# A two-layer convolutional decoder on eight cores: matmuls of constants in the opening, halved first weight loads, LayerNorm steps spread over two tiles, and a buffer of its own for the last short convolution

## The chip, the cores and the metric

The kernel runs on all 8 NeuronCores of one Trainium2 chip. Each core works on one of eight prompts and on 16 of the 128 sample tokens, with all weights, and the cores exchange nothing. The metric is device time in microseconds of the slowest core. Engines are named as in the profile: PE is TensorE, DVE is VectorE, ACT is ScalarE, POOL is GpSimd, SP is SyncE. POOL and SP also issue the DMA transfers: POOL those with a cast to bf16 (weights) and x tiles 1 to 4, SP and ACT the others.

## The reference

Activations are `D_MODEL = 1024` wide, the prompt has 2048 tokens, the hidden width is `D_FF = 2816`. Two layers, each `x += 0.5*SwiGLU1(RMSNorm(x)); x += Mixer(RMSNorm(x)); x += 0.5*SwiGLU2(RMSNorm(x))`, then a final RMSNorm.

```python
def rms_norm(x, g):
    return x * lax.rsqrt(jnp.mean(x * x, axis=-1, keepdims=True) + RMS_EPS) * g

def swiglu(x, w_gate, w_up, w_down):
    return (jax.nn.silu(x @ w_gate) * (x @ w_up)) @ w_down

def conformer_conv_mixer(x, buf, w_pw1, b_pw1, w_dw, b_dw, ln_g, ln_b, w_pw2, b_pw2):
    a, g = jnp.split(x @ w_pw1 + b_pw1, 2, axis=-1)
    c, new_buf = causal_dwconv(a * jax.nn.sigmoid(g), buf, w_dw)      # width 31
    c = jax.nn.silu(layer_norm(c + b_dw, ln_g, ln_b))
    return c @ w_pw2 + b_pw2, new_buf

def short_gated_conv_mixer(x, buf, w_in, w_conv, w_out):
    b_gate, c_gate, h = jnp.split(x @ w_in, 3, axis=-1)
    c, new_buf = causal_dwconv(c_gate * h, buf, w_conv)               # width 3
    return (b_gate * c) @ w_out, new_buf
```

## The kernel before

The activations X lie in SBUF for the whole run, as 8 chunks of 128 features by 2064 tokens, cut into five tiles of 412 to 416 tokens (`TILES`). Every product is a group of 8 (or 6) bf16 matmuls of 128x128 by 412 columns into one PSUM bank, weights streamed through a ring of six slots (`WRing`) whose loads are issued on POOL in the order of use as slots come free.

The order of every engine's instructions is written out by hand: the Python program emits them in sequence, each engine runs its own in that order, and `P.wait` puts semaphore waits between them.

**RMSNorm.** The class `Norm` makes it: squares on ACT (`sq_chunk`), a running sum of the 8 chunks on POOL, one matmul with `ONES` that sums over the features and spreads the result (`part1b`), `rstd` on ACT (Ln, then Exp), and eight `apply` on DVE, one for each chunk, which PE's products wait for chunk by chunk. `queue_norm` puts a tile's steps in the list `later`, and `pump(n)` takes up to n `apply` from it, after each product.

**The opening** (`start_group`). x tile 0 comes in four pieces on SP, tile 1 and 2 in two pieces each and 3 and 4 in one on POOL. The first load of weights waits for x tile 0's second piece. The sums of squares of tiles 0 to 2 are made on PE, eight matmuls of `ONES` by the squares (`pieces_in`), without POOL. Then products (hj, ti), hidden chunk by token tile: (0,0), (1,0), the norm of tile 1, (0,1), (1,1), (2,0), (3,0), the norm of tile 2, and so on. A product (hj, ti) is 8 matmuls with the gate weights (L584) and 8 with the up weights (L590); its gate is a Silu on ACT and a multiplication on DVE (L601). Six banks rotate, two to a product.

**The first mixer's last stage.** While the depthwise convolution's last chunks are normalised (LayerNorm: `z_mean` and `z_rstd` on DVE, two chunks at a time, then Silu on ACT), the product with `w_pw2` runs: `pw2_item(ti, m)` is 8 matmuls (L939) and an update of X on DVE (L945). During tiles 1 and 2 only four banks rotate, so a product waits for the update four products back. `tail_step(m)` places the rest of the LayerNorm after the products of tile 1, and the next norm's squares and sums are emitted between them.

**The second mixer.** For each chunk c: products with the C and H columns, u = C*h (DVE) into `UR[:, c % 2]`, `conv_stage` (ACT copies u, scaled, into TR, L1154, DVE adds two taps, L1161 and L1169) and, one chunk later, `y_stage` (the product with the B columns, times TR, on DVE, L1186). After the last chunk the output product (`bout_item`, L1236) begins. TR is one buffer, so the copy of chunk 7 waits for `y_stage(6)`.

**The end.** The final norm writes X, and each pair of chunks is stored; in the last tile chunks 6 and 7 go singly.

## Time and profile before

| | |
|---|---|
| median of 3 runs | 2380.83 us (2380.26 to 2380.9) |
| the profiled execution, time / span | 2380.29 us / 2378.5 us (slowest core, core 5) |
| spans of the eight cores | 2372.1 to 2378.5 us |
| granted clock of PE, mean | 0.995 to 0.996 |
| busy: PE / DVE / ACT / POOL | 2336.4 / 937.6 / 576.8 / 442.1 us |

The views are all of core 5. PE's busy time is modelled, so a group of matmuls shows its last one longer than it is; distances between starts are the better measure. The row of a wait gives what released the engine as far as the semaphores show. PEclk is the granted clock, 1.00 being 2.4 GHz and 0.50 1.2 GHz.

### The profile page before, as it was taken

The page shows a single profiled execution, that of the slowest core. Times are in us where ns is not written, and L with a number is a line of the kernel's source. Part 1 is how long each engine was busy: PE and PEld are TensorE (multiplying, and loading weights), DVE is VectorE, ACT ScalarE, POOL GpSimd, SP SyncE. Part 2 cuts the span into 40 slices and gives each one's busy share as a digit, 9 for nine tenths or more (in the row PEclk, how much of TensorE's full clock was granted, in tenths as well). Part 3 has the DMA queues.
Part 4 walks back from the last instruction along what each step waited for, and adds up shares of the span by engine and source line. Part 5 has one row for each costly group of instructions (what it writes and reads, how often), then busy time and mean ns, then how long its engine had stood idle before and what let it go on. Part 6 is the DMA issues. An engine that isn't in the chain of part 4 may idle for free.

```text
span 2378.5 us, 33574 instructions; the slowest of 8 cores (2372.1 to 2378.5 us)
## 1 busy us (share of the span) xinstructions
PE 2336.4 (98%) x14218; PEld 1293.1 (54%) x14218; DVE 937.6 (39%) x1613; ACT 576.8 (24%) x1027; POOL 442.1 (19%) x462
## 2 busy tenths in 40 slices
PE   6999999999999999999999999999999999999997
PEld 2555555555545555555555555555555555555554
DVE  2342232374577242232352423225655634224226
ACT  3401101342475101101341010113322420110123
POOL 1300000340565000000340000004200510000014
PEclk9999999999999999999999999999999999999999
DMA  9243323348402253423333334331434144234325
GB/s 210 31 56 36 45 27 36 36 58 171 81 2 36 27 54 36 44 29 36 37 41 36 40 37 51 36 38 18 56 36 37 20 52 50 33 36 49 35 25 143
DMA packets 187174, 116.44 MB, mean 49 GB/s; under 512 B 8208, under 2 KB 184496, under 8 KB 187024
## 3 DMA queue, kind: packets, MB, share of 16 engines
q0 software_dynamic: 167968, 90.66, 33.2%
q1 hardware_dynamic: 18640, 22.99, 3.6%
q8 instruction: 112, 1.84, 0.3%
q10 hardware_dynamic: 416, 0.64, 0.1%
q14 instruction: 38, 0.31, 0.0%
HBM read 183.29 MB, written 14.88 MB: 83 GB/s over the span
## 4 chain that ended last, share of the span: by engine, by line
PE 93%; DVE 3%; ACT 2%; DMA 1%; POOL 1%; issue 1%; DVEq 0%; SPq 0%; POOLq 0%; ACTq 0%
PE ps L590 26%; PE ps L584 26%; PE ps L629 24%; PE ps L1113 7%; PE ps L1236 2%; PE ps L756 2%; PE ps L750 2%; PE ps L997 2%; PE ps L939 2%; DVE arena L460 1%; DMA arena<-ffn_w_up 0%; PE ps L843 0%; DVE arena L881 0%; DVE arena L632 0%; ACT arena L393 0%
## 5 line engine op out<-in xcount | busy, mean ns | idle before, releaser
L584 PE MATMUL ps<-arena 128*128 128x412 bf16 (+1 forms) x3520 | 693.6, 339 | 8.4 <-DVE arena L460 8.2
L590 PE MATMUL ps<-arena 128*128 128x412 bf16 (+1 forms) x3520 | 688.9, 339 | 1.1 <-DMA arena<-ffn_w_up 1.1
L601 DVE TENSOR_TENSOR arena<-arena,ps 128x412 bf16<-128x412 f32 (+1 forms) x440 | 256.9, 584 | 930.8 <-ACT arena L599 930.7
L629 PE MATMUL ps<-arena 128*128 128x412 bf16 (+1 forms) x3520 | 618.8, 338 | 0.0
L599 ACT ACTIVATE arena<-ps 128x412 f32<-128x412 f32 (+1 forms) x440 | 226.6, 515 | 1352.7 <-PE ps L590 1352.6
L584 PEld LDWEIGHTS ps<-arena 128*128 128x128 bf16 x3520 | 344.9, 98 | 286.7 <-DVE arena L460 15.4
L590 PEld LDWEIGHTS ps<-arena 128*128 128x128 bf16 x3520 | 345.1, 98 | 272.8 <-issue 2.7
L629 PEld LDWEIGHTS ps<-arena 128*128 128x128 bf16 x3520 | 343.7, 98 | 270.5
L632 DVE SCALAR_TENSOR_TENSOR arena<-ps,arena 128x412 f32<-128x412 f32 (+1 forms) x480 | 280.4, 586 | 241.9 <-PE ps L629 241.5
L401 POOL TENSOR_TENSOR arena<-arena 128x412 f32<-128x412 f32 (+3 forms) x222 | 236.2, 1064 | 203.8 <-ACT arena L393 186.6
L460 DVE SCALAR_TENSOR_TENSOR arena<-arena,ps 128x412 bf16<-128x412 f32 (+3 forms) x280 | 170.3, 636 | 92.0 <-ACT ps L453 92.0
L393 ACT ACTIVATE arena<-arena 128x412 f32<-128x412 f32 (+1 forms) x254 | 133.8, 545 | 181.2 <-DVE arena L632 94.4
L1113 PE MATMUL ps<-arena 128*128 128x412 bf16 (+1 forms) x960 | 167.8, 338 | 0.0
L271 POOL DMA_DIRECT2D arena<-ffn_w_gate x44 | 39.0, 887 | 644.0 <-PE ps L590 435.3
L271 POOL DMA_DIRECT2D arena<-ffn_w_down x48 | 41.1, 862 | 588.2 <-PE ps L590 588.2
L1113 PEld LDWEIGHTS ps<-arena 128*128 128x128 bf16 x960 | 93.8, 98 | 73.8
L271 POOL DMA_DIRECT2D arena<-ffn_w_up x44 | 38.9, 885 | 187.1 <-PE ps L629 181.9
L997 PE MATMUL ps<-arena 128*32 128x512 bf16 x1088 | 64.3, 380 | 0.3 <-DVE arena L914 0.3
L939 PE MATMUL ps<-arena 128*128 128x412 bf16 (+1 forms) x320 | 59.9, 344 | 4.7 <-DVE arena L945 4.7
L756 PE MATMUL ps<-arena 128*128 128x412 bf16 (+1 forms) x320 | 62.4, 338 | 0.0
L750 PE MATMUL ps<-arena 128*128 128x412 bf16 (+1 forms) x320 | 62.4, 338 | 0.0
L1236 PE MATMUL ps<-arena 128*128 128x412 bf16 (+1 forms) x320 | 56.7, 338 | 1.8 <-DVE arena L1186 1.8
(79 smaller groups left out, 785.9 us busy)
## 6 DMA issues: line engine op xcount, KB each, us to landing
arena<-ffn_w_gate POOLq DMA_DIRECT2D x44, 512.0 KB, 8.3
arena<-ffn_w_up POOLq DMA_DIRECT2D x44, 512.0 KB, 10.4
arena<-ffn_w_down POOLq DMA_DIRECT2D x32, 512.0 KB, 8.9
yT<-arena SPq DMA_DIRECT2D x16, 412.0 KB, 4.7
arena<-ffn_w_down POOLq DMA_DIRECT2D x16, 384.0 KB, 8.2
arena<-a_w_pw POOLq DMA_DIRECT2D x12, 512.0 KB, 11.5
arena<-b_w_in POOLq DMA_DIRECT2D x12, 512.0 KB, 9.3
vb<-arena SPq DMA_DIRECT2D x8, 512.0 KB, 5.5
```

The source lines that it names most:

```text
L271: tk = P.emit("pool", (lambda e, dst=dst, src=src: e.dma_start(out=dst, in_=src)), waits=[ftk] + gate, sem="w%d" % slot, amount=16)
L393: a = P.emit("act", (lambda e, m=m, t0=t0, w=w, buf=buf: e.activation(out=buf[:, 0:w], in_=X[:, m, t0:t0 + w], func=AF.Square)), waits=[tk ...
L401: self.add_tk[ti, m] = P.emit("pool", (lambda e, w=w, buf=buf, acc=acc, accb=accb, last=last: e.tensor_tensor(out=accb[:, 0:w] if last els ...
L460: d = P.emit("dve", (lambda e, c=c, t0=t0, w=w, dst=dst, gcol=self.gcol, bank=self.rs_bank: e.scalar_tensor_tensor(out=dst[:, c, t0:t0 + w ...
L584: P.emit("pe", (lambda e, k=k, jj=jj, t0=t0, w=w, bg=bg, wgv=wgv: e.matmul(psum[:, bg, 0:w], wgv[:, k, jj * 128:(jj + 1) * 128], XN[:, k, ...
L590: pk = P.emit("pe", (lambda e, k=k, jj=jj, t0=t0, w=w, bu=bu, wuv=wuv: e.matmul(psum[:, bu, 0:w], wuv[:, k, jj * 128:(jj + 1) * 128], XN[: ...
L599: a = P.emit("act", (lambda e, s=s, w=w, bg=bg: e.activation(out=ST[:, s, 0:w], in_=psum[:, bg, 0:w], func=AF.Silu)), waits=[pk, st_free[s]])
L601: dd = P.emit("dve", (lambda e, s=s, w=w, bu=bu, hj=hj, t0=t0: e.tensor_tensor(out=HB[:, hj, t0:t0 + w], in0=ST[:, s, 0:w], in1=psum[:, bu ...
L629: pk = P.emit("pe", (lambda e, jj=jj, mm=mm, t0=t0, w=w, b=b, wdv=wdv, n=n: e.matmul(psum[:, b, 0:w], wdv[:, jj, mm * 128:(mm + 1) * 128], ...
L632: dd = P.emit("dve", (lambda e, m=m, t0=t0, w=w, b=b: e.scalar_tensor_tensor(out=X[:, m, t0:t0 + w], in0=psum[:, b, 0:w], scalar=0.5, in1= ...
L997: pk = P.emit("pe", (lambda e, j=j, g=g, c=c, b=b, sl=sl, n=n: e.matmul(psum[32 * g:32 * g + 32, b, :], DGW[:, sl * 4 + g, j, :], V4[:, c ...
L1113: pk = P.emit("pe", (lambda e, k=k, cc=cc, t0=t0, w=w, bk=bk, wv=wv: e.matmul(psum[:, bk, 0:w], wv[:, k, cc * 128:(cc + 1) * 128], XN[:, k ...
```

## The change

Six edits, taken together.

1. **Opening, weights.** `first_pair` loads the first two weight blocks (g0, u0) by halves of 128 columns, in the order g0, u0, g0, u0, all gated on the first piece of x tile 0 instead of the second. Product (0, ti) waits for the first halves only.
2. **Opening, PE.** `pieces_in` is split: `pieces_sq` (ACT) and `pieces_sum` (PE). After the sums of each piece `warm_up(n)` issues n matmuls of constants (`ONES` by `ONES`) into a bank that nobody reads: 5, 2, 2, 6 after the pieces of tile 0, 0 and 10 for tile 1, none for tile 2. Tile 2's squares are issued two products earlier, all eight `apply` of a tile directly after its `rstd`; the squares of tiles 3 and 4 and the sum of tile 3 one product (or more) earlier.
3. **Squares.** The ring of buffers in `sq_chunk` runs on over the tiles, and chunk 0 takes a ring buffer too, instead of the accumulator. Chunk 0's square no longer waits for the last add of the tile before.
4. **First mixer's last stage.** `tail_step` runs over 16 products (tiles 1 and 2) instead of 8, with at most one call of `ln_dve` each; the norms of tiles 0 and 1 are queued later, and two places without an `apply` stand behind their `rstd`.
5. **Second mixer.** The last short convolution writes into the other half of UR instead of TR (`t_of`).
6. **End.** Chunks 6 and 7 of the last tile are stored as a pair, and ACT issues the pairs (0,1) and (4,5), SP the other two.

```diff
+        def first_pair(self, gate):
+            for half in range(2):
+                for v in range(2):
+                    src, shape, _ = self.units[v]
+                    dst = slot_view(v, shape)
+                    c0 = half * 128
+                    tk = P.emit("pool", (lambda e, dst=dst, src=src, c0=c0: e.dma_start(
+                        out=dst[:, :, c0:c0 + 128], in_=src[:, :, c0:c0 + 128])),
+                        waits=[gate], sem=("w%d" if half else "wh%d") % v, amount=16)
...
-        if ti < 4:
+        if ti == 1:
+            W.first_pair(ld_x[0, 0])
+        elif ti < 4:
...
+        for j in range(n):
+            tk = P.emit("pe", (lambda e, b=b, w=w: e.matmul(
+                psum[:, b, 0:w], ONES, ONES[:, 0:1].broadcast_to([128, w]), start=True, stop=True)),
+                sem="auto" if j == n - 1 else None)
...
-            buf = self.ring[:, 0 if m == 0 else 1 + (m - 1) % nr, :]
+            n = self.nsq
+            self.nsq += 1
+            buf = self.ring[:, 1 + n % nr, :]
...
-            guard = acc_free[0] if m == 0 else (self.add_tk.get((ti, m - nr)) if m > nr else acc_free[0])
+            guard = self.used[n - nr] if n >= nr else acc_free[0]
...
-        norm_in(0)
-        need(0)
+        nrm.pieces_sq(0)
+        norm_in(0, (5, 2, 2, 6))
+        nrm.pieces_sq(1)
         acquire(0)
         waiting = [products(hj, 0) for hj in (0, 1)]
-        norm_in(1)
-        need(1)
+        norm_in(1, (0, 10))
...
-        squares = {7: (3, 0), 9: (3, 4), 10: (4, 0), 12: (4, 4)}
-        sums = {12: 3, 14: 4}
+        squares = {5: (3, 0), 7: (3, 4), 9: (4, 0), 11: (4, 4)}
+        sums = {11: 3, 14: 4}
         for i, (hj, ti) in enumerate(order):
             gate(*products(hj, ti))
+            if i == 1:
+                nrm.pieces_sq(2)
             if i == 3:
-                norm_in(2)
+                norm_in(2, (0, 0))
...
+                if jj == 0:
+                    ltg, ltu = W.half_tk.get(ug, ltg), W.half_tk.get(uu, ltu)
...
-        def tail_step(m):
-            if m == 0:
+        TAIL_LN = {3: 2, 4: 3, 6: 4, 7: 5, 8: 6, 9: 7, 10: 8}
+
+        def tail_step(k):
+            if k == 0:
...
-            elif m == 2:
-                ln_dve(PH - 1, 2)
-            else:
-                for c_ in {3: (3,), 4: (4,), 5: (5, 6), 6: (7, 8)}.get(m, ()):
-                    ln_dve(PH - 1, c_)
-                    ln_act(PH - 1, c_)
+            elif k in TAIL_LN:
+                ln_dve(PH - 1, TAIL_LN[k])
+                if k > 3:
+                    ln_act(PH - 1, TAIL_LN[k])
...
-            sums = {(2, 0): 0, (3, 0): 1, (4, 1): 2, (4, 7): 3}
+            sums = {(2, 3): 0, (3, 2): 1, (4, 1): 2, (4, 7): 3}
...
-                if ti == 1:
-                    tail_step(m)
+                if ti < 3:
+                    tail_step((ti - 1) * KC + m)
                 pump(1)
                 if (ti, m) in sums:
-                    queue_norm(nxt, sums[ti, m])
+                    queue_norm(nxt, sums[ti, m], 2 if ti == 2 else 0)
...
+        def t_of(c):
+            return TR_A if c < KC - 1 else UR[:, c % 2 ^ 1, :]
...
-                out=TR, in_=UR[:, ub, :], func=AF.Copy, scale=WCB[:, c, 2:3])), waits=[du, t_free[0]])
+                out=TR, in_=UR[:, ub, :], func=AF.Copy, scale=WCB[:, c, 2:3])),
+                waits=[du, t_free[0], ubl_tk] if c < KC - 1 else [du, u_free[1 - ub], ubl_tk])
```

The third argument of `queue_norm` (`rest`) adds that many empty entries behind the norm's `rstd`; each uses up one `pump`.

## Rows read from the trace of the kernel before

**Rows 1.** The page's busy times: engine, busy us, share, instructions.

```profile
PE 2336.4 (98%) x14218; PEld 1293.1 (54%) x14218; DVE 937.6 (39%) x1613; ACT 576.8 (24%) x1027; POOL 442.1 (19%) x462
```

**Rows 2.** Waits of PE, whole span: us in total, times, longest.

```profile
PE ps L421 <- ACT arena L416: 11.3, 6, 5.6
PE ps L584 <- DVE arena L460: 8.2, 12, 4.2
PE ps L939 <- DVE arena L945: 4.7, 3, 3.1
```

**Rows 3.** Timeline, first 90 us: start, us, engine, line, operation, [idle before].

```profile
8.60 1.04 POOL L271 DMA_DIRECT2D arena<-ffn_w_gate  x1 [7.91 <-DMA arena<-xT]
...
8.95 0.87 PE L421 MATMUL ps<-arena 128*128 128x412 bf16 x2 [2.49 <-ACT arena L416]
...
16.52 2.90 PE L584 MATMUL ps<-arena 128*128 128x412 bf16 x8 [4.17 <-DVE arena L460]
...
25.57 1.58 ACT L416 ACTIVATE arena<-arena 128x1648 bf16<-128x1648 f32 x1 [1.07 <-DMA arena<-xT]
...
27.18 1.56 PE L421 MATMUL ps<-arena 128*128 128x412 bf16 x8
...
30.02 4.52 DVE L460 SCALAR_TENSOR_TENSOR arena<-arena,ps 128x412 bf16<-128x412 f32 x8 [11.86 <-ACT ps L453]
...
30.72 0.35 PE L584 MATMUL ps<-arena 128*128 128x412 bf16 x1 [1.99 <-DVE arena L460]
...
41.23 1.56 PE L584 MATMUL ps<-arena 128*128 128x412 bf16 x8
...
47.48 3.03 ACT L416 ACTIVATE arena<-arena 128x1648 bf16<-128x1648 f32 x2
...
51.91 2.05 PE L584 MATMUL ps<-arena 128*128 128x412 bf16 x8
...
53.80 1.56 PE L590 MATMUL ps<-arena 128*128 128x412 bf16 x8
...
88.45 0.35 PE L584 MATMUL ps<-arena 128*128 128x412 bf16 x1 [0.21 <-DVE arena L460]
```

**Rows 4.** Windows: PE, PEld, DVE, ACT, POOL busy (x), PEclk, DMA share, GB/s.

```profile
30.70:34.60 3.90, 3.15 (x7) 0.71 (x8) 3.90 (x8) 1.51 (x3) 0.00 (x0) 0.72 1.03 266
...
725.73:729.00 3.27, 3.27 (x11) 1.49 (x12) 3.27 (x7) 1.62 (x3) 2.25 (x3) 0.54 0.00 0
...
733.00:745.50 12.50, 12.50 (x73) 6.99 (x72) 9.71 (x17) 5.95 (x12) 8.01 (x8) 1.00 0.01 2
```

**Rows 5.** DMA queues in 4.6:8, 10.5:16.4, 1676.5:1679 (x, weights, sB): packets, MB, share.

```profile
q1 hardware_dynamic: 463, 0.72, 89.9%
...
q0 software_dynamic: 1513, 0.77, 116.4%
...
q1 hardware_dynamic: 1040, 0.13, 32.5%
```

**Rows 6.** Timeline, the first mixer's last stage.

```profile
706.11 1.21 DVE L871 SCALAR_TENSOR_TENSOR arena<-ps,arena 128x1024 f32<-128x1024 f32 x1
...
718.32 4.35 PE L939 MATMUL ps<-arena 128*128 128x412 bf16 x24 [1.37 <-DVE arena L945]
...
721.99 1.28 ACT L448 ACT_TABLE_LOAD   x1
...
725.04 0.64 DVE L945 SCALAR_TENSOR_TENSOR arena<-ps,arena 128x412 f32<-128x412 f32 x1
...
725.73 7.21 PE L939 MATMUL ps<-arena 128*128 128x412 bf16 x32 [3.06 <-DVE arena L945]
```

**Rows 7.** Timeline, end of the second mixer's convolutions.

```profile
1839.57 2.48 DVE L1161 SCALAR_TENSOR_TENSOR arena<-arena 128x1536 f32<-128x1536 f32 x2 [1.99 <-ACT arena L1154]
...
1845.62 4.69 PE L1236 MATMUL ps<-arena 128*128 128x412 bf16 x26 [1.75 <-DVE arena L1186]
```

**Rows 8.** DMA queue in 2368:2371 (the last outputs).

```profile
q1 hardware_dynamic: 431, 0.66, 109.4%
```

More of the change, by code:

```diff
@@ L379, in __init__ @@
             self.tail_sq = None
+            self.nsq = 0
+            self.used = {}
         def sq_chunk(self, ti, m, tk):
@@ L398, in sq_chunk @@
             acc = self.ring[:, 0, :]
+            a0, in0, n0 = self.sq[ti, m - 1]
+            if m > 1:
+                in0 = acc
             accb = self.accb.get(ti, ACCB)
             bfree = accb_free.get(ti in self.accb) if last else None
-            self.add_tk[ti, m] = P.emit("pool", (lambda e, w=w, buf=buf, acc=acc, accb=accb, last=last: e.tensor_tensor(
-                out=accb[:, 0:w] if last else acc[:, 0:w], in0=acc[:, 0:w], in1=buf[:, 0:w], op=ALU.add)),
-                waits=[self.sq[ti, 0], a, self.add_tk.get((ti, m - 1)), bfree])
+            self.add_tk[ti, m] = self.used[n] = P.emit("pool", (
+                lambda e, w=w, buf=buf, in0=in0, acc=acc, accb=accb, last=last: e.tensor_tensor(
+                    out=accb[:, 0:w] if last else acc[:, 0:w], in0=in0[:, 0:w], in1=buf[:, 0:w], op=ALU.add)),
+                waits=[a0, a, self.add_tk.get((ti, m - 1)), acc_free[0] if m == 1 else None, bfree])
+            if m == 1:
+                self.used[n0] = self.used[n]
             if last:
@@ L406, in sq_chunk, with pieces_sq, pieces_sum @@
                 self.sq[ti] = self.add_tk[ti, m]
-        def pieces_in(self, ti):
+        def pieces_sq(self, ti):
+            t0, w = TILES[ti]
+            n = KC // X_PIECES[ti]
+            self.sq_in = []
+            for j in range(X_PIECES[ti]):
+                c0 = j * n
+                self.sq_in.append(P.emit("act", (lambda e, t0=t0, w=w, c0=c0, n=n: e.activation(
+                    out=SQ[:, c0:c0 + n, 0:w], in_=X[:, c0:c0 + n, t0:t0 + w], func=AF.Square)),
+                    waits=[ld_x[ti, j], sq_free[0]]))
+        def pieces_sum(self, ti, warm):
             t0, w = TILES[ti]
@@ L413, in pieces_in @@
             p1 = None
-            for j in range(X_PIECES[ti]):
-                c0 = j * n
-                a = P.emit("act", (lambda e, t0=t0, w=w, c0=c0, n=n: e.activation(
-                    out=SQ[:, c0:c0 + n, 0:w], in_=X[:, c0:c0 + n, t0:t0 + w], func=AF.Square)),
-                    waits=[ld_x[ti, j], sq_free[0]])
-                P.wait("pe", a)
-                for c in range(c0, c0 + n):
-                    p1 = P.emit("pe", (lambda e, c=c, w=w, bank=bank: e.matmul(
-                        psum[:, bank, 0:w], ONES, SQ[:, c, 0:w], start=(c == 0), stop=(c == KC - 1))),
-                        sem="auto" if c == KC - 1 else None)
+            for c in range(KC):
+                if c % n == 0:
+                    P.wait("pe", self.sq_in[c // n])
+                p1 = P.emit("pe", (lambda e, c=c, w=w, bank=bank: e.matmul(
+                    psum[:, bank, 0:w], ONES, SQ[:, c, 0:w], start=(c == 0), stop=(c == KC - 1))),
+                    sem="auto" if c == KC - 1 else None)
+                if c % n == n - 1:
+                    warm_up(warm[c // n])
             sq_free[0] = p1
@@ L477, in build_program, with queue_norm @@
     later = collections.deque()
-    def queue_norm(nrm, ti):
+    def queue_norm(nrm, ti, rest=0):
         later.append((nrm, ti, -1))
+        for _ in range(rest):
+            later.append((nrm, ti, KC))
         for c in range(KC):
```

49 lines of the change are left out of this document (33 added, 16 removed).

## The prediction, on record before the changed kernel ran

> **What bounds the kernel now.** I read first the busy table of the page: TensorE (PE) is busy for 98% of the span [rows 1], so a change can only win PE's idle time and the time in which PE's clock stands at its lower level. Next the list of waits, which says where PE idles [rows 2]: in the first sums of squares (11.3 us, waiting for ScalarE's squares), before products that wait for VectorE's `apply` (8.2 us), and at three places of the first mixer's last stage (4.7 us); the timeline adds one of 1.75 us before the second mixer's output product [rows 7]. Waits ahead of the first product are mostly the transfers' anyway, so the sum is not to be had whole. I therefore read the timeline at each place [rows 3, 6, 7], and the windows for the clock [rows 4]. A full-rate matmul of 412 columns costs 12.50/73 = 0.17 us, at clock 0.54 it costs 3.27/11 = 0.30 us [rows 4], so at the lower level (1.2 of 2.4 GHz) about 0.34 us. A product (8+8 matmuls) is 2.8 us at full rate, a group of 8 is 1.4 us.
>
> **First group, tiles 0 and 1.** Before: weights are asked for at 8.60 us, PE's first product starts at 16.52, its 8 matmuls taking 2.90 us, the lower level. The second half of x tile 1 is seen at 25.57, the eight sums run from 27.18 to 28.74, and the first product of tile 1 starts at 30.72 [rows 3]: 2.0 us of `rstd` and the first `apply`. The next eight matmuls go at VectorE's pace (eight `apply` in 4.52 us, 0.56 each [rows 3]), the clock falls on the way (0.72 over the stretch) [rows 4], and product (2,0) starts at 41.23 [rows 3].
>
> After: the four weight transfers may start when the first piece of x tile 0 is in, at the first square, some 3.4 us earlier. But the DMA engines were not idle then: queue 1 used 89.9% of them for x tile 0 [rows 5]. The order of bytes changes, their sum does not, so x tile 1's end, which starts the chain to (0,1), can only win what was slack: one tenth of 4 to 7 us, plus what two queues do together (share 116% with one software queue [rows 5]). I take 2.0 us. Against it stand the extra packets of the halves. A packet of the whole pair takes 16 x 5.9 us x 1.164 / 1513 = 73 ns; one of sB's (128 bytes) takes 16 x 2.5 us x 0.325 / 1040 = 12.5 ns [rows 5]. The pair has 2 x 1024 packets, the halves 4 x 1024 with half the bytes. Lower bound: cost goes by bytes alone, 0 us extra. If a packet costs 4 ns and the rest by bytes, 2048 x 4 / 16 = 0.5 us. Upper bound: each half packet costs the whole 73 ns, 2048 x 73 / 16 = 9.3 us. Since 128 bytes cost 12.5 and 512 bytes written cost 73, the price follows bytes closely; I take 0.6 us. Net x tile 1 is 1.4 us earlier. The first product itself starts earlier and at whatever clock ends before the sums of tile 1 can run, so its clock buys almost nothing more: a product pair (24 matmuls at the lower level costing 24 x 0.17 = 4.1 us more) now stands in slack.
>
> The Trainium skill's page DMA: Bandwidth & Descriptors (Specifications) says that transfers under 512 bytes fall below line rate because the DMA engine then reads, modifies and writes; the halves write 256 bytes. The sB row, 12.5 ns for 128 bytes written to SBUF, does not show such a penalty; by the rule the halves would be nearer my upper bound, which stands as a rival below.
>
> Constants' matmuls: 15 in tile 0 lie in waits of PE. Five at 0.34 us are 1.7 us, in a wait that was 2.49 us [rows 3], and the next piece comes later now, since it shares the engines; six after the last sum are at most 2.1 us beside the `rstd` chain of 2.0 us. Cost 0, at most 0.1. The ten of tile 1 cost 1.7 us at full rate, hidden in the 2.0 us chain; at the lower level 3.4 us, which would cost 1.4 us. What they buy: PE enters the paced eight with no idle time behind it. Paced at 0.17 in 0.56 us, PE is still only 30% active, and the trace of before has no such stretch without a gap ahead of it. Bounds: the clock falls as before, 0; it never falls, and 12 to 16 matmuls save 0.17 us each, 2.1 us, up to 2.7. I take the middle, 1.1. Tiles 0 and 1 together: 1.4 + 1.1 = 2.5 us, from -0.5 to 5.
>
> **Tile 2.** Before, its squares start at 47.48, after (3,0)'s gate; PE has finished (3,0) at 41.23 + 4 x 1.4 = 46.8, waits, sums, and runs the first half of (2,1) from 51.91 at the lower level; the second half starts at 53.80 [rows 3]. After, the squares are issued after gate (1,1), some 6 us earlier; they end near 42, before PE is done with (3,0). PE then needs 1.4 (sums) + 1.4: 49.6 instead of 53.80, a gain of 4.2. The eight `apply` now all come ahead of gate (2,1), and (0,2) may wait 0.2 us for the last. New queueing: ScalarE now waits for x tile 2's transfer with gates (2,0) and (3,0) behind it. PE has six banks, three products or 8.4 us, so the transfer must be over 6 us late to matter. I take 4.0 (3 to 4.2).
>
> **Tiles 3 and 4.** PE waited three times at 88.45 and after for `apply` of tile 3, 0.2 us each, the first of them shown [rows 3]. Its sum now goes one product (2.8 us) earlier: 0.6 us gained. The squares of tile 3, one or two products earlier, may wait on their transfer; three products of banks cover it.
>
> **First mixer's last stage.** Here PE waits 1.37 us at 718.32 and 3.06 us at 725.73, and 0.3 once [rows 2, 6], then does its next matmuls at clock 0.54 until 729.0 (3.27 us, 11 matmuls, where 11 x 0.17 = 1.9 would do) [rows 4]: 4.7 + 1.4 = 6.1 us. Cause: four rotating banks, and VectorE does an update (0.56 us) plus up to four LayerNorm steps (1.21 us, of which some 0.08 overlaps the step before, as with the `apply` of 0.64: 1.13 each) inside one 1.4 us product; then the first `apply` of tile 0 blocks VectorE on a `rstd` whose table load only starts at 721.99, so the update that frees the bank comes at 725.04 [rows 6]. After: the eight steps stand over products k = 3 to 10 (counted from the first of tile 1), with k = 4 the only one with two. VectorE's work for k = 2 to 10 is 9 x 0.56 + 8 x 1.13 = 14.1 us against PE's 9 x 1.4 = 12.6. Starting near 705.5 (just before the step at 706.11 [rows 6]), I work out that it does the update of k = 10 near 719.0; PE wants that bank for k = 14 at 720.6. The tightest margin is k = 15, about 1.2 us. `rest=2` puts two updates between `rstd` and the first `apply`, so an `apply` that waits holds up an update that PE needs five products later. ScalarE's square of chunk 0 no longer waits for the last add. Tile 3's products need the last Silu (worked out the same way: VectorE 720.2, ScalarE about 721.7) at 723.4. The last stage's `apply` work ends five products later; it spills into the next FFN, where VectorE has 2.8 us a product for one gate (0.58) and four `apply` (2.2). It is full there for four products, and tile 2 is finished about 2 us ahead of its use. I take 6.0 (4 to 6.2).
>
> **Last short convolution.** The copy that starts the taps waited for the last product with the old TR, and VectorE for the copy, 1.99 us, until 1839.57; PE waited 1.75 us, until 1845.62 [rows 7]. With its own buffer the copy starts 6.5 us earlier, VectorE goes from the last product straight to the taps, 2.0 us earlier; the gain is PE's whole wait, 1.75 (1.5 to 1.8).
>
> **Final output.** The last four issues become two pairs on each queue. The engines were 109% in use by one queue in 2368 to 2371 [rows 8], so bytes decide; the last pair has twice the bytes of the single chunk but ScalarE's queue works one pair earlier. I take 0.2 gained (-0.7 to 1).
>
> **The sum.** 2.5 + 4.0 + 0.6 + 6.0 + 1.75 + 0.2 = 15.0 us. The profiled execution took 2380.3 us around its span of 2378.5, the median of the runs is 2380.8, 0.5 more. So 2380.8 - 15.0 = 2365.8 us.
>
> **Rivals.**
> (A) Half packets cost like whole ones, 73 ns: x tile 1 and everything behind it 8.7 us later than in my sum, 2374.5 us. For it: with a cast the cost may go by packet. Against: 12.5 ns for sB's. 10%.
> (B) The same mechanism ends slower than before if a half packet costs well over a whole one: 4096 x p / 16 against 9.3 us; at p = 97 ns the gain of 15 is gone, at p = 146 (twice a whole one) the extra is 28 us, 12.5 more than the gain, 2393 us. No row is near that. 2%.
> (C) The wait in the mixer moves instead of going: VectorE, full through the next FFN's first four products, is late with tile 2 or 3. PE then waits about 3 us and may do 16 matmuls at the lower level, 2.7 us: 2371.5 us. Against: 2 us of margin. 13%.
> (D) The opening wins only tile 2: x tile 1 lands no earlier and the clock falls in the paced stretch as before: 2.5 less, 2368.3 us. For it: the DMA engines' shares [rows 5]. 25%, inside my range.
> (E) More: both queues together carry x better and the clock stays up: 3 to 4 us more, 2362 us. 15%.
> My forecast has 35%, within 2 us.
>
> **How the numbers follow.** From the forecast to (D) and (E), and to just past (C), the range is 2361.5 to 2372.0. Left out are (A), (B) and the ends of (C) and (E), near 20%. A difference under 0.2% (4.8 us) can't be told from no change. Faster by more than that: the forecast, (C), (D), (E) and most of (A), 0.93. Within 0.2%: (A) together with part of (C) or (D), 0.05. Slower: (B), 0.02.
>
> **What would show it.** In the changed profile: squares of x tile 1's second half at 24 to 25 us (30 or more speaks for A); no PE wait at the sums of tile 2 and no clock below 1.00 around it; no wait of PE's L939-type products for VectorE and the clock at 1.00 throughout the mixer's last stage; no wait of the output product of the second mixer; in the next FFN no wait for `apply` over 0.5 us (C otherwise). If the DMA stream of the opening is over 3 us longer, or PE shows a new wait at the FFN after the mixer, the prediction is wrong.

## The result and the profile after

The profiled execution of the changed kernel took 2366.11 us (a second run 2366.08), against 2380.26 to 2380.9 before: ratio 0.994, 95% interval 0.9916 to 0.9964, faster by 14.5 us or 0.6%. The prediction was 2365.8. The spans of the cores are 2362.7 to 2364.5 us, the slowest is core 1 with 2364.5, and the granted clock is 0.995 to 0.997. Core 5, from which the rows of before are, went from 2378.5 to 2363.6 us (14.9), the slowest core from 2378.5 to 2364.5 (14.0), the mean of the eight from 2376.09 to 2363.71 (12.4). Two further runs of the changed kernel (2412.18 and 2524.28 us), most runs of the experiments and all of the last version had four or all of their cores at a lower granted clock (means of 0.82 to 0.99), so there only the four cores of the undisturbed half are used, and of the two runs with whole first loads only the opening. When x tile 1 arrives is the transfers' matter and is taken over all eight cores.

The busy table and the waits of PE of the changed kernel, core 1 [rows 1, 2]; the columns of the waits are total us, times, longest:

```profile
PE 2333.9 (99%) x14243; PEld 1294.1 (55%) x14243; DVE 936.6 (40%) x1613; ACT 577.9 (24%) x1027; POOL 443.2 (19%) x464
```

```profile
PE ps L469 <- ACT arena L456: 10.0, 5, 5.8
PE ps L640 <- DVE arena L510: 2.7, 13, 0.2
PE ps L489 <- ACT arena L419: 2.6, 1, 2.6
PE ps L640 <- DMA arena<-ffn_w_gate: 1.8, 1, 1.8
PE ps L1053 <- DMA arena<-vb: 1.2, 1, 1.2
PE ps L899 <- POOL arena L883: 0.7, 2, 0.4
```

Lines have moved: L469 is the sum of squares (L421 before), L640 and L646 the gate and up products (L584, L590), L995 the first mixer's output product (L939). 8.2 us of waits for `apply` have become 2.7, none longer than 0.2, and the 4.7 us before the mixer's output product are gone altogether. Two lines deserve a look because nothing in the change names them: L489 waits 2.6 us for the last square (core 5 before: 1.59), and L1053, the depthwise convolution, waits 1.2 us for a relay load.

The timeline of the opening, changed kernel, core 1 [rows 3]:

```profile
5.41 1.04 POOL L283 DMA_DIRECT2D arena<-ffn_w_gate  x1 [4.71 <-DMA arena<-xT]
...
6.41 1.92 PE L397 MATMUL ps<-arena 128*128 128x412 bf16 x5
...
14.65 1.15 PE L640 MATMUL ps<-arena 128*128 128x412 bf16 x4 [1.80 <-DMA arena<-ffn_w_gate]
...
26.45 1.58 ACT L456 ACTIVATE arena<-arena 128x1648 bf16<-128x1648 f32 x1 [1.42 <-DMA arena<-xT]
...
28.08 1.55 PE L469 MATMUL ps<-arena 128*128 128x412 bf16 x4 [2.13 <-ACT arena L456]
29.43 2.56 PE L397 MATMUL ps<-arena 128*128 128x412 bf16 x10
30.92 4.52 DVE L510 SCALAR_TENSOR_TENSOR arena<-arena,ps 128x412 bf16<-128x412 f32 x8 [13.31 <-ACT ps L503]
...
35.68 1.56 PE L646 MATMUL ps<-arena 128*128 128x412 bf16 x8
...
39.86 1.56 PE L640 MATMUL ps<-arena 128*128 128x412 bf16 x8
40.53 3.03 ACT L456 ACTIVATE arena<-arena 128x1648 bf16<-128x1648 f32 x2
...
45.44 1.56 PE L469 MATMUL ps<-arena 128*128 128x412 bf16 x8
46.83 1.56 PE L640 MATMUL ps<-arena 128*128 128x412 bf16 x8
48.22 1.56 PE L646 MATMUL ps<-arena 128*128 128x412 bf16 x8
```

The weights are asked for 3.2 us earlier than on core 5 before and the first product begins 1.9 us earlier, but PE then waits again, for the second half of x tile 1, and that is not earlier. Tile 2's squares are done in time (40.53), its sums (45.44) and its first product (46.83) follow without a gap. The constants' ten matmuls (29.43) lie in the wait for `rstd`. The windows show the clock behind them (columns as in [rows 4]):

```profile
28.00:30.50 2.50, 2.42 (x8) 1.08 (x9) 0.00 (x0) 0.76 (x3) 0.00 (x0) 0.50 1.30 190
30.50:34.50 4.00, 3.17 (x14) 1.17 (x12) 3.58 (x7) 2.59 (x4) 0.00 (x0) 0.97 1.05 288
34.50:38.00 3.50, 3.09 (x17) 1.53 (x17) 2.04 (x5) 0.51 (x1) 0.00 (x0) 1.00 1.09 216
```

PE had been at the lower level (0.50, 1.2 GHz), and on this core is back at 2.4 GHz for the paced stretch (the eight matmuls that go at the pace of `apply`) that before had a mean of 0.72.

The first mixer's last stage, in the timeline and in the windows of the changed kernel, core 1 [rows 4, 6]:

```profile
698.18 15.50 PE L995 MATMUL ps<-arena 128*128 128x412 bf16 x88
713.70 14.10 PE L995 MATMUL ps<-arena 128*128 128x412 bf16 x80
```

```profile
706.00:722.00 16.00, 16.00 (x94) 9.00 (x92) 13.38 (x20) 13.69 (x23) 10.83 (x11) 1.00 0.00 2
722.00:745.00 23.00, 23.00 (x134) 12.83 (x132) 17.57 (x31) 12.37 (x22) 16.80 (x17) 1.00 0.00 1
```

There is no idle time between the groups, and the clock is 1.00 in both windows. At the end of the second mixer the product at the output starts without an idle bracket [rows 7]:

```profile
1818.77 1.99 ACT L1214 ACTIVATE arena<-arena 128x2048 f32<-128x2048 f32 x1
...
1825.39 2.48 DVE L1222 SCALAR_TENSOR_TENSOR arena<-arena 128x1536 f32<-128x1536 f32 x2
...
1831.60 13.57 PE L1298 MATMUL ps<-arena 128*128 128x412 bf16 x77
```

**The whole account.** The program was cut at marks that both kernels have, each interval taken from starts in the trace, mean over the eight cores. "Second half" of a product is its group of eight up matmuls; each row runs from the mark of the row above:

| interval | before | after | gain | forecast |
|---|---|---|---|---|
| start to second half of x tile 1 (its square starts) | 26.62 | 26.91 | -0.3 | 1.4 |
| to second half of product (2,0) | 16.03 | 14.75 | 1.3 | 1.1 |
| to second half of (2,1) | 10.44 | 6.97 | 3.5 | 4.0 |
| to the first down product | 69.16 | 67.95 | 1.2 | 0.6 |
| to the last matmul of the depthwise convolution | 574.61 | 575.20 | -0.6 | 0 |
| to the first product of the next FFN | 55.21 | 48.65 | 6.6 | 6.0 |
| the two FFNs | 923.29 | 923.28 | 0.0 | 0 |
| second mixer, first product to output product | 169.61 | 167.70 | 1.9 | 1.75 |
| to the last down product | 517.90 | 518.05 | -0.2 | 0 |
| to the last sum of squares | 2.29 | 3.48 | -1.2 | 0 |
| to the end | 10.93 | 10.79 | 0.1 | 0.2 |
| span | 2376.09 | 2363.71 | 12.4 | 15.0 |

The spread of the cores is large in the first row: the square starts between 24.40 and 29.08 us before, between 25.96 and 28.36 after. Core 5 gained 1.3 us up to (2,0) and 4.2 from there to (2,1). The fourth row can be taken apart by product, and comes out alike on all eight cores: the first eight matmuls of (0,2) took 1.92 us instead of 2.38, those of (0,3) 1.39 instead of 2.61, those of (0,4) 2.82 instead of 2.36. So tile 3 gained 1.2 us, tile 2 0.5, and tile 4 lost 0.5.

### The profile page after: what moved, and what is told of

The parts are those of the page before. It is cut to its first block, busy times and chain, and to the rows that moved or that the text cites. A ratio compares the mean times of both kernels' runs of the same rounds, so it can differ in the third digit from the quotient of the medians.

```text
span 2364.5 us, 33719 instructions; the slowest of 8 cores (2362.7 to 2364.5 us)
## 1 busy us (share of the span) xinstructions
PE 2333.9 (99%) x14243; PEld 1294.1 (55%) x14243; DVE 936.6 (40%) x1613; ACT 577.9 (24%) x1027; POOL 443.2 (19%) x464
## 4 chain that ended last, share of the span: by engine, by line
PE 94%; DVE 2%; DMA 2%; ACT 1%; POOL 0%; issue 0%; SPq 0%; DVEq 0%; POOLq 0%; ACTq 0%
PE ps L646 25%; PE ps L640 25%; PE ps L685 24%; PE ps L1168 7%; PE ps L995 2%; PE ps L812 2%; PE ps L1298 2%; PE ps L806 2%; DVE arena L510 2%; PE ps L1053 2%; DMA arena<-xT 1%; PE ps L899 0%; DMA arena<-vb 0%; DVE arena L688 0%; DMA vb<-arena 0%
## 5 line engine op out<-in xcount | busy, mean ns | idle before, releaser
L640 PE MATMUL ps<-arena 128*128 128x412 bf16 (+1 forms) x3520 | 689.5, 338 | 4.7 <-DVE arena L510 2.7
L646 PE MATMUL ps<-arena 128*128 128x412 bf16 (+1 forms) x3520 | 687.3, 338 | 0.0
L640 PEld LDWEIGHTS ps<-arena 128*128 128x128 bf16 x3520 | 343.6, 98 | 279.6 <-DVE arena L510 10.4
L646 PEld LDWEIGHTS ps<-arena 128*128 128x128 bf16 x3520 | 344.8, 98 | 270.3 <-issue 1.3
L688 DVE SCALAR_TENSOR_TENSOR arena<-ps,arena 128x412 f32<-128x412 f32 (+1 forms) x480 | 280.7, 587 | 242.5 <-PE ps L685 242.3
L510 DVE SCALAR_TENSOR_TENSOR arena<-arena,ps 128x412 bf16<-128x412 f32 (+3 forms) x280 | 170.4, 638 | 85.4 <-ACT ps L503 85.4
L1053 PE MATMUL ps<-arena 128*32 128x512 bf16 x1088 | 64.2, 380 | 1.2 <-DMA arena<-vb 1.2
L995 PE MATMUL ps<-arena 128*128 128x412 bf16 (+1 forms) x320 | 58.1, 338 | 0.0
## 6 DMA issues: line engine op xcount, KB each, us to landing
arena<-b_w_in POOLq DMA_DIRECT2D x12, 512.0 KB, 10.4
```

The lines of the kernel that those rows point to most:

```text
L510: d = P.emit("dve", (lambda e, c=c, t0=t0, w=w, dst=dst, gcol=self.gcol, bank=self.rs_bank: e.scalar_tensor_tensor(out=dst[:, c, t0:t0 + w ...
L640: P.emit("pe", (lambda e, k=k, jj=jj, t0=t0, w=w, bg=bg, wgv=wgv: e.matmul(psum[:, bg, 0:w], wgv[:, k, jj * 128:(jj + 1) * 128], XN[:, k, ...
L646: pk = P.emit("pe", (lambda e, k=k, jj=jj, t0=t0, w=w, bu=bu, wuv=wuv: e.matmul(psum[:, bu, 0:w], wuv[:, k, jj * 128:(jj + 1) * 128], XN[: ...
L688: dd = P.emit("dve", (lambda e, m=m, t0=t0, w=w, b=b: e.scalar_tensor_tensor(out=X[:, m, t0:t0 + w], in0=psum[:, b, 0:w], scalar=0.5, in1= ...
L1053: pk = P.emit("pe", (lambda e, j=j, g=g, c=c, b=b, sl=sl, n=n: e.matmul(psum[32 * g:32 * g + 32, b, :], DGW[:, sl * 4 + g, j, :], V4[:, c ...
```

## The experiments

Each differs from the changed kernel by the edit shown. "x tile 1" means the start of its second square, on which the chain to product (0,1) hangs.

### The first loads whole, the early gate kept

```diff
-            for half in range(2):
-                for v in range(2):
...
+            for v in range(2):
+                src, shape, _ = self.units[v]
+                dst = slot_view(v, shape)
+                tk = P.emit("pool", (lambda e, dst=dst, src=src: e.dma_start(out=dst, in_=src)),
+                            waits=[gate], sem="w%d" % v, amount=16)
```

> The changed kernel with the first two weight blocks loaded whole again, still gated on the first piece of x tile 0. Theory (a packet costs by its bytes: the half packets took no longer per byte, 0.76 MB in 5 us of the changed kernel's trace against 0.77 MB in 5.9 us before): the second half of x tile 1 comes within 0.5 us of the changed kernel's mean over the cores (26.9 us), product (2,0) starts within 0.5 us of 40.3; only the first product starts later, by 1 to 3 us, in slack. Span change under 0.5 us. Rival (packets have a price of their own): x tile 1 comes 1 to 5 us earlier, and so does (2,0).

x tile 1 came at 25.62 us in the mean of the eight cores, 1.3 us earlier than in the one profile of the changed kernel. The same kernel was run again on another chip:

> The kernel with whole first loads (gated on the first piece) once more, since the first run of it was disturbed behind its opening. That run's opening had the second half of x tile 1 at 25.6 us in the mean over the cores, against 26.9 to 27.6 in four profiles with halves. Theory (2048 more packets have a price of their own, some 12 ns each): again 25.3 to 26.0 us. Rival (chance: cores vary by 4 us): 26.5 to 27.5. For the span: the halves' theory that they help PE gives 0 to 1 us longer with whole loads, since (1,0) is done later; the rival, that x tile 1 decides, 1 us shorter.

Again 25.62 (24.4 to 26.4). Against it stand seven profiles of kernels with halves and the early gate (the changed one and six of those below that leave these transfers as they are): 26.91, 27.04, 27.14, 27.19, 27.45, 27.61 and 27.63, mean 27.28. So the halves cost 1.66 us, and 16 x 1.66 / 2048 = 13 ns for each extra packet, where I had taken 4.

A rival for the 1.66 us is POOL: it issues four weight transfers instead of two, 0.9 us each, so x tile 1 itself is asked for at 9.9 us instead of 8.2. The packet records speak against it. With halves and with whole loads (means over the cores) the first weight packet starts at 9.5 to 9.7 us and x tile 1's first at 16.0 to 16.7, over 6 us after its issue. From the first weight packet to the last of x tile 1 the engines move 3.2 to 3.3 MB in either case, in 15.3 and 15.6 us with whole loads, at 210 GB/s, and in 16.8 to 17.6 us with halves, at 187 to 191. It is the rate that is lower.

The queue of weights in 11 to 16 us of the changed kernel, core 1 [rows 5]:

```profile
q0 software_dynamic: 2946, 0.76, 159.0%
```

The bytes are the same as before in a like stretch (0.77 MB), in twice the packets: 16 x 5 us x 1.59 / 2946 = 43 ns for a half packet, against 73 for a whole. If a packet costs a + b x bytes, the two give a = 13 ns. That this is the same number is partly chance: with shares over 100% the packets of an engine overlap, so their times are no sum of its time, and over the whole pair of loads and all cores a half packet took 44 to 45 ns and a whole one 70 to 75, which gives a = 14 to 19. By all this the fixed part is 13 to 19 ns, where I had taken 4. In bytes written the window has 6.0 for each ns of packet time, against 7.0 for whole packets. The Trainium skill says (DMA: Bandwidth & Descriptors, Specifications) that transfers under 512 bytes fall short of line rate. The sign agrees, by 15%; a price that would make half packets as dear as whole ones, my rival A, is not to be seen.

The halves do buy an earlier first product, but it runs into the wait for x tile 1. The first down product began at 115.95 us in the mean of the six cores with whole loads whose clock was at 1.00 from (2,0) up to it (2 to 5 of the first run, 6 and 7 of the second), and at 116.99 us in the mean of the thirty such cores of six profiles with halves and the constants' matmuls (the changed kernel alone: 116.58). So the halves by themselves cost 1.0 us; the other 0.6 of the 1.66 are lost again between x tile 1 and (2,0), and why stays open.

### The gate on the second piece of x tile 0

```diff
-            W.first_pair(ld_x[0, 0])
+            W.first_pair(ld_x[0, 1])
```

> The changed kernel with the first weights gated on the second piece of x tile 0 again. Theory (the DMA engines had slack before, about 1 us, and the early gate used it: with whole loads x tile 1 came at 26.6 with the late gate and 25.6 with the early one): the second half of x tile 1 at 28.0 to 28.6 us in the mean over undisturbed cores instead of 27.3, (2,0) later by the same. Rival (the engines are never idle, so the gate moves only the order): 27.0 to 27.5.

x tile 1 at 28.22 us, so the earlier gate is worth 28.22 - 27.28 = 0.9 us with halves. Whole loads with the late gate (the kernel before) are at 26.62, with the early one at 25.62: 1.0. Both agree, though each rests on one profile with the late gate, and half of my 2.0 us was not there.

### No constants' matmuls

```diff
-        norm_in(0, (5, 2, 2, 6))
+        norm_in(0, (0, 0, 0, 0))
...
-        norm_in(1, (0, 10))
+        norm_in(1, (0, 0))
```

> The changed kernel with no matmuls of constants at all. Theory (they keep the clock at 2.4 GHz through the eight paced matmuls of (0,1)): the clock falls in that stretch as before, the second half of (0,1) runs at 0.34 us a matmul, product (2,0) starts 1.5 to 2.5 us later than in the changed kernel, so does everything behind it: 1.5 to 2.5 us longer. Rival (the earlier start of PE's real work does it): clock 1.00 and no change, within 0.5 us.

From x tile 1 to the second half of (2,0) 15.79 us instead of 14.75: 1.04 us, between the two expectations; 1.1 us when the stretch is followed to the first down product. The clock is what changed. Without them, core 6, timeline and windows:

```profile
32.81 4.41 PE L640 MATMUL ps<-arena 128*128 128x412 bf16 x8 [1.99 <-DVE arena L510]
37.01 2.95 PE L646 MATMUL ps<-arena 128*128 128x412 bf16 x8
```

```profile
30.50:34.50 4.00, 1.93 (x5) 0.34 (x4) 2.39 (x5) 3.32 (x5) 0.00 (x0) 0.50 1.12 281
34.50:38.00 3.50, 3.38 (x8) 0.98 (x9) 3.12 (x6) 0.00 (x0) 0.00 (x0) 0.50 1.05 243
```

Eight matmuls take 2.95 us instead of 1.56, after an idle time of 1.99 us. Part of this hides: the first eight are paced by `apply`, and the cost comes with the eight behind them, up to 8 x 0.17 = 1.4 us, and on core 6 another 0.5 us in the eight after those. The eight cores took 14.74 to 16.80 us for the interval, against 14.43 to 14.81 with the constants.

The granted clocks of all cores tell how. In the kernel before, every core was at 1.00 in the sums of tile 1 and fell to 0.50 in the paced stretch. In the changed kernel PE waited twice for squares in these sums on every core (0.3 to 2.5 us), before at most once, and every core was at 0.50 by their end. It was at 1.00 before the second eight matmuls of (0,1) began; without the constants every core was still at 0.50 there. So the constants didn't keep a high clock up, as I had thought, they brought a low one back earlier. Which of the 25 do it, the ten of tile 1 or the fifteen of tile 0 too, was not tried. The span of the eight cores is 2361.9 to 2366.3 us, mean 2364.2, 0.5 more than with the constants, where 1.5 to 2.5 was expected; the other rows differ by as much between two profiles.

### The old last stage of the mixer

The old `tail_step` on tile 1 alone, and the old places of the norms; the new ring of buffers stays.

```diff
+            else:
+                for c_ in {3: (3,), 4: (4,), 5: (5, 6), 6: (7, 8)}.get(m, ()):
+                    ln_dve(PH - 1, c_)
+                    ln_act(PH - 1, c_)
...
-            sums = {(2, 3): 0, (3, 2): 1, (4, 1): 2, (4, 7): 3}
+            sums = {(2, 0): 0, (3, 0): 1, (4, 1): 2, (4, 7): 3}
...
-                    queue_norm(nxt, sums[ti, m], 2 if ti == 2 else 0)
+                    queue_norm(nxt, sums[ti, m])
```

> The changed kernel with the first mixer's last stage as before: tail_step over tile 1 only, norms queued after products (2,0) and (3,0), no empty entries. Theory (VectorE's order makes PE wait): waits of 1.4 and 3 us and the lower clock are back, from the last convolution matmul to the next FFN's first 55.2 us instead of 48.7, 6.0 to 6.5 us longer in all. Rival (the ring of squares, which stays changed, was the cause of the late rstd): under 3 us longer.

The stage took 52.51 us, against 48.65 (changed) and 55.21 (before). So 3.9 us come with the placement, and 2.7 of the 6.6 were gained by what else had changed, of which only the ring acts in this stage: a miss for both expectations. On core 4 PE waits as long as before the first time (1.37 us in [rows 6]), but 1.65 instead of 3.06 us the second:

```profile
715.14 4.35 PE L995 MATMUL ps<-arena 128*128 128x412 bf16 x24 [1.38 <-DVE arena L1001]
...
721.14 5.75 PE L995 MATMUL ps<-arena 128*128 128x412 bf16 x32 [1.65 <-DVE arena L1001]
```

The shorter wait also left the clock at 1.00: the 32 matmuls behind it took 5.75 us, where core 5 before has 7.21 [rows 6]. 1.4 us of wait and 1.5 us of clock together are about the 2.7.

### Only the norms at their old places

The spread LayerNorm steps stay; the two empty places behind `rstd` go too, so they are not told apart from the places of the norms.

```diff
-            sums = {(2, 3): 0, (3, 2): 1, (4, 1): 2, (4, 7): 3}
+            sums = {(2, 0): 0, (3, 0): 1, (4, 1): 2, (4, 7): 3}
...
-                    queue_norm(nxt, sums[ti, m], 2 if ti == 2 else 0)
+                    queue_norm(nxt, sums[ti, m])
```

> The changed kernel with the LayerNorm steps spread as they are now, but the norms of tiles 0 and 1 queued after products (2,0) and (3,0) as before and no empty entries. From the last convolution matmul to the next FFN's first: 48.65 with both, 52.5 with neither. Theory (the apply that blocks VectorE on a late rstd is the cause): 51 to 52.5. Rival (the bunched LayerNorm steps are the cause, the place of the norm is free): 48.6 to 49.5.

51.5 to 51.6 us on cores 4 to 7: 2.9 us for the placement of the norms, and so 52.51 - 51.55 = 1.0 us for spreading the LayerNorm steps. Core 4 shows the chain, ACT, DVE, then PE:

```profile
712.87 1.28 ACT L498 ACT_TABLE_LOAD   x1
...
715.35 0.64 DVE L510 SCALAR_TENSOR_TENSOR arena<-arena,ps 128x412 bf16<-128x412 f32 x1 [2.80 <-ACT ps L503]
715.91 0.64 DVE L1001 SCALAR_TENSOR_TENSOR arena<-ps,arena 128x412 f32<-128x412 f32 x1
...
716.61 1.57 PE L995 MATMUL ps<-arena 128*128 128x412 bf16 x8 [1.88 <-DVE arena L1001]
```

The `apply` (L510) stands first in DVE's queue and waits 2.80 us for a `rstd` that begins with a table load; the update (L1001) that frees the bank waits behind it, and PE behind that.

### The old choice of buffers for the squares

```diff
-            buf = self.ring[:, 1 + n % nr, :]
+            buf = self.ring[:, 0 if m == 0 else 1 + (m - 1) % nr, :]
...
-            guard = self.used[n - nr] if n >= nr else acc_free[0]
+            guard = acc_free[0] if m == 0 else (self.add_tk.get((ti, m - nr)) if m > nr else acc_free[0])
```

> The changed kernel with the square's buffers chosen as before: chunk 0 into the accumulator, the ring started anew in each tile. Theory (in the last tile, with three ring buffers, the fourth square now waits for the first add, ScalarE is late with the rstd of tile 3, and VectorE with the last updates): the time from the last output matmul of FFN 4 to the last sum of squares goes from 3.5 us back to 2.3, and the run is 1.0 to 1.2 us shorter, nothing else moves. Rival (the last tile's delay comes from elsewhere, and the running ring pays in the mixer's last stage): no gain at the end, and a new wait of PE in the mixer's last stage.

The mixer's last stage is 48.65 us, unchanged to the hundredth: with the norms placed late the ring is worth nothing, though it was worth 2.7 us beside the old placement. Both act on the same wait, the late `rstd`. And the end is shorter: 2.43 us from the last down product to the last sum, instead of 3.48; the mean span is 2362.75, 0.96 less. The changed kernel's last tile, core 1, ACT, then DVE and PE:

```profile
2343.69 1.55 ACT L429 ACTIVATE arena<-arena 128x416 f32<-128x416 f32 x3 [1.06 <-DVE arena L688]
2346.04 0.55 ACT L429 ACTIVATE arena<-arena 128x416 f32<-128x416 f32 x1 [0.80 <-POOL arena L441]
2346.50 0.59 ACT L498 ACTIVATE arena<-ps,arena 128x412 f32<-128x412 f32 x1
...
2347.67 0.64 DVE L510 SCALAR_TENSOR_TENSOR arena<-arena,ps 128x412 f32<-128x412 f32 x1 [2.58 <-ACT ps L503]
2348.23 0.58 DVE L688 SCALAR_TENSOR_TENSOR arena<-ps,arena 128x416 f32<-128x416 f32 x1
...
2352.61 0.70 PE L489 MATMUL ps<-arena 128*128 128x416 bf16 x3 [2.62 <-ACT arena L419]
```

With the old choice, core 0, the four squares go in one group and the same sum waits 0.9 us less:

```profile
2345.40 1.87 ACT L429 ACTIVATE arena<-arena 128x416 f32<-128x416 f32 x4 [1.35 <-POOL arena L441]
...
2353.28 0.70 PE L489 MATMUL ps<-arena 128*128 128x416 bf16 x3 [1.72 <-ACT arena L419]
```

Chunk 0 used to lie in the accumulator, so that four squares fitted ahead of the first add. Now it takes one of the three ring buffers, the fourth square waits for the first add, the previous tile's `rstd` (L498) is queued behind that square on ACT, the `apply` behind `rstd`, the updates of X (L688) behind the `apply` on DVE, and the last square behind them.

### A ring of seven for the final norm

```diff
+    norms[6].ring = view(O_CB, [8, 512], F32)
```

> The changed kernel with a ring of seven buffers for the final norm's squares (in the convolution's area, free by then) instead of three. Theory (the fourth square of the last tile waits for an add): from the last output matmul to the last sum of squares 2.2 to 2.4 us instead of 3.5, 1.1 us shorter. Rival (VectorE's order alone makes it late): 3.5, no change.

2.1 to 2.2 us on cores 4 to 7 instead of 3.48: 1.3 us won, slightly more than with the old choice. The wait on core 4 is now

```profile
PE ps L489 <- ACT arena L419: 1.5, 1, 1.5
```

### The old TR for the last convolution, and single chunks at the end

```diff
-            return TR_A if c < KC - 1 else UR[:, c % 2 ^ 1, :]
+            return TR_A
...
-                if c % 2 == 1:
-                    c0 = c - 1
+                single = ti == NT - 1 and c >= KC - 2
+                if single or c % 2 == 1:
+                    c0 = c if single else c - 1
```

> The changed kernel with two parts undone that lie apart: the last short convolution into TR again, and the last chunks stored singly. Theory for the first (TR's reuse makes the copy late): the second mixer's time from its first product to the output product goes from 167.7 back to 169.6 us. Rival: the copy was hidden, 167.7. Theory for the end (bytes decide): from the last sum to the end 10.0 to 11.0 us in the mean over the cores, as before (10.9) and after (10.8), within 0.3. Rival (a last single chunk lands sooner than a pair): 0.5 us or more shorter.

The second mixer takes 169.7 us on cores 0 to 3, against 167.70: 2.0 us, and the old picture is back on core 0:

```profile
1830.95 2.48 DVE L1223 SCALAR_TENSOR_TENSOR arena<-arena 128x1536 f32<-128x1536 f32 x2 [2.05 <-ACT arena L1215]
...
1837.00 5.21 PE L1299 MATMUL ps<-arena 128*128 128x412 bf16 x29 [1.81 <-DVE arena L1249]
```

The end takes 10.0, 11.1, 10.4 and 11.3 us, mean 10.7, against 10.79 with pairs: no difference in that spread.

### x tile 1 asked for between the halves, and (1,0) beside the `rstd`

If the halves are to pay, x tile 1 must not stand behind them. So it is asked for before the second halves, and product (1,0), whose weights come last, fills the time in which tile 1's `rstd` and `apply` are made.

```diff
+        if ti == 1:
+            W.first_pair(ld_x[0, 0], (1,))
...
-        waiting = [products(hj, 0) for hj in (0, 1)]
-        norm_in(1, (0, 10))
+        waiting = [products(0, 0)]
+        warm_up(8)
+        norm_in(1, (6, 4))
+        waiting.append(products(1, 0))
```

> A version built on what was found: x tile 1 is asked for before the second halves of the first weights, and product (1,0) comes after the sums of tile 1, beside its rstd and apply; 8 matmuls of constants after product (0,0), 6 and 4 after the sums. Theory (x tile 1 sets the opening, PE waits for it and then for VectorE): second half of x tile 1 at 23 to 24.5 us, product (2,0)'s second half at 36.5 to 39 instead of 41.7, the whole 3 to 4.5 us shorter. Rival (the transfers behind become late instead: g2, u2, x tile 2): the second half of (2,1), 48.6 now, moves less than 2 us, and PE waits for weights or for tile 2's squares.

Timeline, core 4:

```profile
21.64 1.58 ACT L459 ACTIVATE arena<-arena 128x1648 bf16<-128x1648 f32 x1 [1.10 <-DMA arena<-xT]
...
26.95 1.57 PE L645 MATMUL ps<-arena 128*128 128x412 bf16 x8
27.47 4.53 DVE L513 SCALAR_TENSOR_TENSOR arena<-arena,ps 128x412 bf16<-128x412 f32 x8 [9.33 <-ACT ps L506]
...
29.75 1.03 PE L645 MATMUL ps<-arena 128*128 128x412 bf16 x5
...
37.81 1.56 PE L651 MATMUL ps<-arena 128*128 128x412 bf16 x8
```

x tile 1 at 22.2 us (mean of cores 4 to 7), the second half of (2,0) near 37.4 instead of 41.66, the first down product at 112.3 instead of 116.58: 4.3 us.

### The same PE order with whole loads

The edit is the PE part of the one above, with the whole loads of the first experiment and the ring of seven.

> e9_best with whole first loads, so x tile 1 comes behind both of them, but product (1,0) still beside the rstd of tile 1. It tells the order of PE's work from the order of the transfers. Theory (both count): x tile 1's second half at 25.6 us, (2,0)'s second half at 38.5 to 39.5, between 41.7 of the changed kernel and 34.6 of e8_order. Rival (PE's order is all): 36.5 or less; rival (the transfers are all): 41 or more.

(The 34.6 in that text is the second half of (1,1) in the kernel above; the figure to compare with is 37.4.) x tile 1 at 25.2 us, (2,0) near 39.3, first down product at 114.2 us on cores 0 to 3. The changed kernel is not the one to compare with, since its loads are halves. Against whole loads in the old order (115.95 us) the place of (1,0), with the constants moved along, is worth 1.8 us; the other 1.0 us towards the thirty cores' 116.99 is that of the whole loads. x tile 1's transfers between the halves give another 1.9 to 2.4 (114.2 less 112.3 of the kernel above, on another chip, and 111.8 of the next, cores 0 to 3), and it is there that the halves pay. Whole loads with x tile 1 asked for between the two were not tried.

### All that held, together

The edit of x tile 1 between the halves, (1,0) beside the `rstd`, and the ring of seven.

> The reordered opening of e8_order and the seven-buffer ring of e7_bigring together. Theory (the two gains lie at opposite ends of the run and add up: 3.8 to 4.3 us at the opening on undisturbed cores, 1.2 to 1.3 at the end): 2361 us, 4.5 to 5.5 under the changed kernel, ratio to the kernel before 0.9915 to 0.992. Rival (what the opening gains goes into a transfer that comes late, such as the relay of the first mixer's convolution, where PE already waited 1 to 2 us on some cores): 2363 us or more.

Core 0 at the end: the fourth square waits 0.22 us, for an update, and the sum 1.49:

```profile
2339.74 0.55 ACT L432 ACTIVATE arena<-arena 128x416 f32<-128x416 f32 x1 [0.22 <-DVE arena L693]
...
2346.30 0.70 PE L492 MATMUL ps<-arena 128*128 128x416 bf16 x3 [1.49 <-ACT arena L422]
```

On cores 0 to 3 of the profiled run the first down product starts at 111.1 to 112.5 us and the last sum of squares comes 2.2 us after the last down product. There is no time of the whole chip to hold against the 2361 us of the text above, only spans of four cores, nine such groups here and eleven of the kernel before on the same chip. The mean span is 2360.2 against 2376.3 us, the slowest core of the four 2361.3 against 2378.1: 16.0 and 16.8 us less than before. The changed kernel by the same measure (five groups) has 2363.7. So both changes together gave 3.5 us more, less than the 4.5 to 5.5 expected; the profiled run alone gave 5.5. The kernel without the ring of seven has 2359.8 (three groups, another chip), so that the ring's 1.3 us add to the span is not shown, though its row of the account shows them, and the two can't be ranked.

## Why the prediction came out

The time was right (2366.1 for 2365.8), and the mechanisms of the three large terms were, in the main; but several terms were off, one was right for another reason, and two losses were not seen. On the average core they cost 2.6 us of the sum of 15.0. That the time came within 0.3 us is therefore partly luck: the metric is the slowest core, and the spans of the eight cores, 6.4 us apart before, were 1.8 us apart after, mostly by when x tile 1 and the last outputs landed on each. Core 5, with which the sum was made, gained 14.9.

- **x tile 1, 1.4 us earlier: wrong.** It was 0.3 us later. "One tenth of 4 to 7 us, plus what two queues do together", taken as 2.0, measured 0.9 to 1.0. "I take 0.6" for the extra packets measured 1.66: the price of a packet does not follow its bytes as closely as the row of sB suggested, 13 ns are its own. The squares at 24 to 25 us that I named as the sign did not appear. Rival A (a half packet costs like a whole one) is as clearly wrong: 9.3 us was its price.
- **The clock, 1.1 us: right in size**, 1.04, and there by luck: no reason was given for the middle of the bounds, and the mechanism was another. I had PE enter the paced stretch at the high clock and keep it. On all eight cores the clock was at 0.50 by the end of the sums, in which PE now waited twice, and came back to 1.00 in the constants' matmuls (four cores) or within the first eight paced ones (four). What a later return costs is in part hidden under the pace of `apply`.
- **Tile 2, 4.0 us: right**, 3.5 in the mean and 4.2 on core 5, and no wait at its sums. Rival D (the opening wins only tile 2) therefore describes the opening nearly as well as my forecast: tiles 0 and 1 gave 1.0 of 2.5 us.
- **Tiles 3 and 4, 0.6: mis-sized**, 1.2 in tile 3 alone. I priced each of the three waits by its idle time, 0.2 us. But matmuls that wait for `apply` start 0.55 us apart instead of 0.17, so each wait costs 0.38 us, and that is the 1.2. Tile 4, from which I expected nothing, lost 0.5 us, as much as (0,2) gained.
- **The first mixer's last stage, 6.0: right**, 6.6, with no wait and the clock at 1.00. The cause was told right in part. The `apply` that blocks DVE on a late `rstd` is worth 2.9 us (with the new ring) and the density of LayerNorm steps 1.0; the rest of the 6.6 went with the ring, but only while the old placement stood. Their prices overlap and can't be added.
- **Rival C** (the wait moves into the next FFN) did not come: no wait for `apply` in the next FFN is over 0.2 us, and the two FFNs take the same time to 0.01 us.
- **The last short convolution, 1.75: right**, 1.9 to 2.0. **The final output, 0.2:** 0.1, and the pairs themselves make no difference, so nothing was gained here that can be told from the spread of 9.8 to 11.6 us over the cores.
- **Not foreseen: 1.2 us at the last sum.** The ring was costed only where it helps ("no longer waits for the last add"). That it takes away the fourth buffer ahead of the first add was written in the diff.
- **Not foreseen, and open: 0.6 us in the depthwise convolution.** PE waits for the relay load from `vb` on five cores (1.3, 1.2, 0.5, 1.9 and 1.5 us on cores 0, 1, 4, 5 and 6), before on two (0.3 and 1.5). The difference, 4.6 / 8 = 0.6 us in the mean, fits the row of the account. No experiment was made on why; the edits don't touch that transfer. The wait falls on other cores in each profile, in one on none; the kernels without constants, with the old last stage and with the old buffers have 574.9, 574.9 and 575.1 us in this row, against 574.6 before and 575.2 after. With one profile of the kernel before it stays open how much of the 0.6 us is chance.

## What to carry to other kernels

Find the transfer that the chain hangs on, and order both the transfers around it and the products by it: smaller first loads started a product earlier and brought the load that mattered 1.7 us later, until that load was put between them and a product was put beside the `rstd` that it leads to (4.3 us). When a buffer changes its role, count the buffers at each use of the ring, the last tile too, and follow each in-order queue behind the instruction that would wait. Two cures of one wait are tested apart and together, because here the first alone gave 2.7 us and on top of the second nothing.

## What the runs showed of the hardware

A weight packet with a cast took 70 to 75 ns with 512 bytes written and 43 to 45 ns with 256, so 13 to 19 ns of its own beside the bytes. On core 1 the granted clock, at 0.50 before ten matmuls of constants, was 0.97 and then 1.00 in the paced stretch behind them, where PE does one matmul of 0.17 us in every 0.56; without them it stayed at 0.50 to 38 us on core 6. Matmuls that each wait for a step of DVE cost the distance between their starts, 0.38 us more than at full rate, though the idle time shown is 0.21. The start of one and the same square in the opening differs by 4.7 us between the cores of a chip, more than most terms of this sum, so an opening is compared over all cores.
